# Feed-forward in two phases, with the gated tensor kept in DRAM between them

## What is computed

```python
def conv_ffn(h, w_up, conv_w, conv_b, w_down):        # h is 1024 x 1024, D_FF = 2816
    u = causal_dwconv(h @ w_up, conv_w, conv_b)       # w_up 1024 x 5632, three taps
    g, val = jnp.split(u, 2, axis=-1)
    return (jax.nn.silu(g) * val) @ w_down            # w_down 2816 x 1024
...
for layer in range(2):
    h = h + mixer(rms_norm(h, ...))                   # layer 0: RG-LRU and attention, layer 1: mLSTM
    h = h + conv_ffn(rms_norm(h, f_norm_g[layer]), f_w_up[layer], ..., f_w_down[layer])
return rms_norm(h, final_norm_g)
```

## Time and profile before

| | us |
|---|---|
| median of 3 runs | 2327.4 |
| lowest, highest | 2326.35, 2329.44 |
| span of the profiled execution | 2324.5 |
| feed-forward of layer 0, first to last matmul | about 484.7 to 1172.7 |
| feed-forward of layer 1 | about 1614.9 to 2303.3 |

### The profile page before, as it was taken

The page is one execution under the profiler, slowest core; times in us unless marked ns, Lnnn a source line. Parts: engine busy times, 40 slices in busy tenths (PEclk is TensorE's granted clock), DMA queues, the critical chain, the costliest instruction groups (busy, mean ns, idle before and its releaser), DMA issues.

```text
span 2324.5 us, 31827 instructions
## 1 busy us (share of the span) xinstructions
PE 2264.2 (97%) x10415; PEld 1844.0 (79%) x10415; DVE 1334.6 (57%) x2179; ACT 903.4 (39%) x1595; POOL 1029.8 (44%) x713
## 2 busy tenths in 40 slices
PE   8999998999999999999999999999999999999997
PEld 6776777878888888888878878878888888888885
DVE  6946655268655555555661115664975555555556
ACT  5635554134333333333431124451443333333333
POOL 2314433423555555555533332223345555555554
PEclk9999999999999999999999999999999999999998
DMA  5100001301111111111231110021101111111112
GB/s 179 44 19 1 1 0 30 125 28 46 55 55 55 54 49 45 51 54 54 64 127 46 45 36 28 28 100 55 46 19 55 55 55 54 54 47 51 47 54 91
DMA packets 34583, 122.07 MB, mean 53 GB/s; under 512 B 3840, under 2 KB 3968, under 8 KB 34240
## 3 DMA queue, kind: packets, MB, share of 16 engines
q1 hardware_dynamic: 31616, 106.44, 14.8%
q10 hardware_dynamic: 2880, 14.49, 1.6%
HBM read 112.52 MB, written 8.39 MB: 52 GB/s over the span
## 4 chain that ended last, share of the span: by engine, by line
PE 79%; DVE 8%; ACT 4%; issue 3%; POOL 3%; DMA 2%; ACTq 0%; SPq 0%; DVEq 0%; POOLq 0%
PE ps L736 8%; PE ps L738 8%; PE ps L737 8%; PE ps L818 7%; PE ps L816 7%; PE ps L814 7%; PE ps L854 6%; PE ps L856 6%; PE ps L855 6%; PE ps L1573 2%; DMA stage<-in_wt 2%; POOL wlo L516 2%; PE ps L1738 1%; PE ps L1740 1%; PE ps L1742 1%
## 5 line engine op out<-in xcount | busy, mean ns | idle before, releaser
L516 POOL TENSOR_TENSOR wlo<-stage,whi 128x512 fp32r<-128x512 f32 x308 | 397.3, 1295 | 460.3 <-ACT whi L979 455.7
L736 PE MATMUL ps<-ahi,whi 128*128 128x512 f32 x896 | 368.5, 411 | 17.7 <-DVE alo L2263 10.4
L435 POOL TENSOR_TENSOR whi<-stage,cons 128x1024 fp32r<-128x1024 f32 x64 | 124.5, 1945 | 540.0 <-PE ps L738 329.1
L738 PE MATMUL ps<-ahi,wlo 128*128 128x512 f32 x896 | 351.3, 392 | 0.0
L737 PE MATMUL ps<-alo,whi 128*128 128x512 f32 x896 | 351.0, 392 | 0.0
L1239 DVE TENSOR_TENSOR hT<-hT,ps 128x512 f32<-128x512 f32 x352 | 238.4, 684 | 157.6 <-PE ps L856 157.6
L979 ACT CAST whi<-stage 128x512 fp32r<-128x512 f32 x308 | 189.1, 620 | 357.9 <-POOL stage L529 182.7
L854 PE MATMUL ps<-hid_hi,whi 128*128 128x512 f32 x640 | 251.8, 393 | 2.9 <-POOL wlo L516 1.9
L856 PE MATMUL ps<-hid_hi,wlo 128*128 128x512 f32 x640 | 249.2, 389 | 0.0
L855 PE MATMUL ps<-hid_lo,whi 128*128 128x512 f32 x640 | 249.1, 389 | 0.0
L814 PE MATMUL ps<-ahi,whi 128*128 128x512 f32 x608 | 236.5, 389 | 0.0
(11 more groups left out here) (323 smaller groups left out, 4083.0 us busy)
## 6 DMA issues: line engine op xcount, KB each, us to landing
stage<-in_wt SPq DMA_DIRECT2D x184, 512.0 KB, 3.7
hT<-in_xt SPq DMA_DIRECT2D x16, 256.0 KB, 6.9
hT<-in_xt ACTq DMA_DIRECT2D x8, 512.0 KB, 7.7
spill<-hT ACTq DMA_DIRECT2D x1, 4096.0 KB, 12.1
hT<-spill ACTq DMA_DIRECT2D x8, 512.0 KB, 8.4
out<-hT SPq DMA_DIRECT2D x16, 256.0 KB, 2.1
wqb_s<-in_wqb ACTq DMA_DIRECT2D x1, 1024.0 KB, 4.9
wlru_s<-in_wlru SPq DMA_DIRECT2D x1, 512.0 KB, 10.7
```

The costliest lines, as they stand in the source:

```text
L516: nc.gpsimd.tensor_tensor(block_lo(c), src, block_hi(c).bitcast(F32), ALU.subtract).then_inc(sem(L + "b_ready"), 1)
L736: nc.tensor.matmul(bank, hi, rhs_k[0][:, tok], start=k_first, stop=False)
L738: return nc.tensor.matmul(bank, lo, rhs_k[0][:, tok], start=False, stop=k_last)
```

## The change

The feed-forward block is made in two phases, in both layers. In the **first** (f = 0 to 3 plain, PF = 4, then 18 steps i of seven products, f = i + 4) only up projection, convolution and gate run. The gated tensor of a pair g, two tiles by two token halves (X11, X12, X21, X22), gets four differences in Strassen's way (`hidden_sums`; XT3 overwrites X12), and the seven pieces `hs` are written to DRAM (`hidden_out`, 1792 KB) into `hops`. `first_down`, `down` and `last_down` are gone. In the **second** phase the down projection runs as seven block products p, each over the 11 pairs: 77 steps n = 11p + g. A step takes one 512-wide weight block and one 512-token piece, and makes 12 matmuls into four PSUM banks, which stay open over the 11 steps of the product, and over several products where these share sums: product 1's banks go on through products 2, 3 and 4, product 5's through 6. After each product DVE adds the four banks to a quarter of `hT` (`evacuate`). Per step SP brings the piece (256 KB) from DRAM through a ring of 8, ACT rounds the weight block and the piece (`down_block`, `operand_hi`), POOL takes the weight's rest (`block_rest`), DVE the piece's (`operand_lo`); both splits go through rings of 4. The weight sums S1 to S4 are made by DVE in place (`weight_sum`), at the steps given by `sums_at`. Raw quarters of the down weights are loaded during products 0 to 1. The stage gets a second pair of tiles. The next norm's first half (tokens 0 to 511) is done within products 5 and 6, its second half begins there; layer 1's first two weight tiles are split by POOL at steps 58 and 62. The loops are unrolled.

```diff
-PLAIN = 8
-DOWN_BANKS, LAST_BANKS = (4, 5, 6), (4, 5, 0, 6)
-BLOCKS = 18 * (FG - 2) + 11
+PF = 4
+PLAIN = 2 * PF
+SF = FT - PF
+UPS = 7 * SF
+STEPS = 7 * FG
+BLOCKS = UPS + STEPS
...
-                nc.tensor.matmul(bank, block_hi(b)[:, wk], hid_hi[:, j, tok], start=(j == 0), stop=False)
-                nc.tensor.matmul(bank, block_hi(b)[:, wk], hid_lo[:, j, tok], start=False, stop=False)
-                return nc.tensor.matmul(bank, block_lo(b)[:, wk], hid_hi[:, j, tok], start=False, stop=(j == 1))
-                    for j in range(2):
-                        mm = down_part(g, q, c, n, n // 2, n % 2, j)
-                        mm.then_inc(b_used, 2)
-                    else:
-                        mm.then_inc(sem(L + "down"), 1)
...
+        hops = nc.dram_tensor("hops", (FG * P, 7 * HALF), F32, kind="Internal").ap()
...
+        steps = [("A12", X21), ("A11", X11), ("S2", XT2), ("S3", XT3), ("A22", XT4), ("S1", XT1), ("S4", X22)]
+        targets = [(0, 0), (0, 0), (0, 1), (4, 1), (4, 0), (4, 1), (0, 1)]
+        chain_banks = [(1, 0, 2, 3)] + 4 * [(4, 5, 6, 7)] + 2 * [(1, 0, 2, 3)]
+        fresh = (0, 1, 5)
...
+        sums_at = {}
+        for g in range(FG):
+            sums_at.setdefault(FG + g + 3, []).extend([("S1", g), ("S2", g)])
+            sums_at.setdefault(2 * FG + g + 3, []).append(("S4", g))
+            sums_at.setdefault(3 * FG + g - 2, []).append(("S3", g))
+        sums_made = [what for n in sorted(sums_at) for what in sums_at[n]]
...
+            def hidden_out(L, g):
+                sp.wait_ge(*counts(L, "h_sum")(4 * (g + 1)))
+                sp.dma_start(hops[g * P:(g + 1) * P, :], hs[:, :, :].rearrange("p a b -> p (a b)")
+                             ).then_inc(sem("h_out"), 16)
+            def hidden_in(L, n):
+                g, what = n % FG, steps[n // FG][1]
+                sp.wait_ge(sem("h_out"), 16 * (FG * LAYER[L] + g + 1))
+                sp.dma_start(x_piece(n), hops[g * P:(g + 1) * P, what * HALF:(what + 1) * HALF]
+                             ).then_inc(x_landed(L, n)[0], 16)
...
+                for n in range(XRING, STEPS):
+                    k = n - XRING
+                    sp.wait_ge(*counts(L, "x_lo")(k + 1))
+                    hidden_in(L, n)
+                    if k < FG:
+                        sp.wait_ge(*b_ready(UPS + k + 1))
+                        raw_in(L, t0, "A11", k)
+                    elif k < 2 * FG:
+                        sp.wait_ge(*b_ready(UPS + k + 1))
+                        raw_in(L, t0, "A21", k - FG)
+                        raw_in(L, t0, "A22", k - FG)
...
+                if i == 0:
+                    pe.wait_ge(sem("t_lo"), t_count(L, "t4", 3))
+                pe.wait_ge(*uv(5 * i + 2))
+                product(q + 4, 2, "T4", False)
+                pe.wait_ge(*ev(2 * i + 1))
+                product(q + 5, 0, "B21", False)
+                pe.wait_ge(*uv(5 * i + 3))
+                product(q + 6, 3, "B22", False)
...
+            def down_step(n):
+                p, g = n // FG, n % FG
+                pe.wait_ge(*b_ready(UPS + n + 1))
+                pe.wait_ge(*counts(L, "x_lo")(n + 1))
+                hi, lo = x_hi[n % 4][:, :], x_lo[n % 4][:, :]
+                for m in range(4):
+                    if g == 0:
+                        if p == 0:
+                            pe.wait_ge(*(uv(5 * SF - 1), ev(2 * SF), uv(5 * SF - 1), uv(5 * SF))[m])
+                        elif p == 1:
+                            pe.wait_ge(*counts(L, "prod")(2 * FT))
+                        elif p == 5:
+                            pe.wait_ge(*dn(4))
+                        else:
+                            pe.wait_ge(*dn(4 * (p - 1) + m + 1))
+                    wm = slice(m * P, (m + 1) * P)
+                    bank = ps[:, chain_banks[p][m], :]
+                    nc.tensor.matmul(bank, block_hi(UPS + n)[:, wm], hi, start=(g == 0 and p in fresh), stop=False,
+                                     skip_group_check=True)
+                    nc.tensor.matmul(bank, block_hi(UPS + n)[:, wm], lo, start=False, stop=False,
+                                     skip_group_check=True)
+                    mm = nc.tensor.matmul(bank, block_lo(UPS + n)[:, wm], hi, start=False, stop=(g == FG - 1),
+                                          skip_group_check=True)
+                    if g == FG - 1 and m < 3:
+                        mm.then_inc(sem("down"), 1)
+                mm.then_inc(sem("b_used"), 1)
...
+            for n in range(STEPS):
+                down_step(n)
+                if n == 5 * FG + 9:
+                    pe_sums(pe, next_norm, 0, sq)
+                if n == 6 * FG + 2:
+                    pe_spread(pe, next_norm, 0, diag)
+            pe.sem_inc(w_used, 3 * FT - PLAIN)
...
+            def operand_hi(n):
+                act.wait_ge(*b_used(UPS - 2 if n < 4 else UPS + n - 3))
+                act.wait_ge(*x_landed(L, n))
+                nc.scalar.copy(x_hi[n % 4][:, :], x_piece(n)).then_inc(sem("x_hi"), 1)
...
+            for n in range(4, STEPS):
+                p, g = n // FG, n % FG
+                down_block(n)
+                operand_hi(n)
+                if p == 5 and 3 <= g <= 6:
+                    square(2 * g - 6, 0)
+                    square(2 * g - 5, 0)
+                if (p, g) == (5, 10):
+                    act_std(act, next_norm, 0)
+                if p == 6 and 3 <= g <= 10 and next_norm != "nf":
+                    act_round(act, next_norm, g - 3)
+                if p == 6 and 4 <= g <= 7:
+                    square(g - 4, 1)
+            for pos in range(4, KT):
+                square(pos, 1)
...
+            def prod(f, s):
+                dve.wait_ge(*counts(L, "silu")(f * 2 + (1 + s)))
+                dve.wait_ge(*counts(L, "conv")(tap_count(f, 1, s)))
+                nc.vector.tensor_tensor(x_at(f, s), x_at(f, s), ps[:, 6 + s, :], ALU.mult
+                                        ).then_inc(sem("prod"), 1)
+            def hidden_sums(g, ns):
+                for n in ns:
+                    dve.wait_ge(*(counts(L, "prod")(4 * g + 4) if n == 0 else counts(L, "h_sum")(4 * g + n)))
+                    out, a, b = ((XT1, X12, X11), (XT3, X22, X12), (XT2, X22, XT1), (XT4, X21, XT2))[n]
+                    nc.vector.tensor_tensor(hs[:, out, :], hs[:, a, :], hs[:, b, :], ALU.subtract
+                                            ).then_inc(sem("h_sum"), 1)
...
+            def operand_lo(n):
+                dve.wait_ge(*counts(L, "x_hi")(n + 1))
+                nc.vector.tensor_tensor(x_lo[n % 4][:, :], x_piece(n), x_hi[n % 4][:, :].bitcast(F32), ALU.subtract
+                                        ).then_inc(sem("x_lo"), 1)
...
+                mix(i, 0)
+                if odd:
+                    hidden_sums(f // 2 - 1, (0, 1))
+                mix(i, 1)
+                if i == 0:
+                    for k in range(4):
+                        t4_lo(k)
+                if odd:
+                    hidden_sums(f // 2 - 1, (2, 3))
+                mix(i, 2)
...
+            def weight_sum(kind, g):
+                a11, a12, a21, a22 = (raw[name][g][:, :] for name in ("A11", "A12", "A21", "A22"))
+                if kind == "S1":
+                    dve.wait_ge(*raw_landed(L, g, 4))
+                    out, a, b, op = a21, a21, a22, ALU.add
+                elif kind == "S2":
+                    dve.wait_ge(*counts(L, "made")(made("S1", g)))
+                    dve.wait_ge(*b_ready(UPS + FG + g + 1))
+                    out, a, b, op = a11, a21, a11, ALU.subtract
+                elif kind == "S4":
+                    dve.wait_ge(*counts(L, "made")(made("S2", g)))
+                    out, a, b, op = a12, a12, a11, ALU.subtract
+                else:
+                    if g >= 2:
+                        dve.wait_ge(*b_ready(UPS + 3 * FG + g - 1))
+                    out, a, b, op = d3_tmp[g % 2][:, :], a22, a11, ALU.subtract
+                nc.vector.tensor_tensor(out, a, b, op).then_inc(sem("made"), 1)
...
+            def evacuate(p, m):
+                k0, s = targets[p]
+                if m < 3:
+                    dve.wait_ge(*counts(L, "down")(3 * p + m + 1))
+                else:
+                    dve.wait_ge(*b_used(UPS + (p + 1) * FG))
+                h = hT[:, k0 + m, halves[s]]
+                nc.vector.tensor_tensor(h, h, ps[:, chain_banks[p][m], :], ALU.add).then_inc(sem("down_read"), 1)
...
+            for n in range(4, STEPS):
+                p, g = n // FG, n % FG
+                operand_lo(n)
+                if p >= 1 and g == 2:
+                    for m in range(4):
+                        evacuate(p - 1, m)
+                for kind, of in sums_at.get(n, ()):
+                    weight_sum(kind, of)
+                if (p, g) == (5, 4):
+                    dve.wait_ge(*counts(L, "down_read")(4 * p))
+                if p == 5 and 4 <= g <= 7:
+                    for pos in (2 * g - 8, 2 * g - 7):
```

(13 more changed lines are left out.)

906 lines of the change are left out of this document (391 added, 515 removed).

## The result

| | before | after |
|---|---|---|
| median, us | 2326.9 | 2362.6 |
| lowest, highest, us | 2325.5, 2329.4 | 2357.9, 2363.2 |
| span of the profiled execution, us | 2324.5 | 2360.3 |
| ratio, 95% interval | | 1.015 (1.0138 to 1.0162) |

The account below looks back on a forecast made before the run. TensorE was taken as the bound: 2324.5 - 69.2 + 17.4 + 4 + 14.2 + 14.3 + 5 = 2310.2 us of span, and with 2.9 more, 2313. The 8-in-10 range was 2272 to 2341.

Parts of the forecast that it names:

- seams between up and down: Up-to-down seams in the feed-forward disappear, 11 per layer at 0.35 to 0.37 us: -8 us.
- begin of layer 1: TensorE's wait at layer 1's begin shrinks as first token half's pieces are ready; second half still awaits last adds: -2 us.
- start of products: Step 0 of the products, both layers: TensorE waits for T4's lo parts, a take-out and a block, 8.7 per layer: +17.4 us.
- hidden differences in the steady steps: Steady first-phase steps: second mix behind two `hidden_sums` is done 0.5 us early, so no cost; bound 16 us in all.
- boundaries between products: Second phase: TensorE waits for adds at p = 2 (2.6), 3 (0.9), 4 (0.5), 6 (3.1): +14.2 us, bounds 4 and 24.
- product 6, layer 0: From step 69, norm and operand splits loop through ScalarE and VectorE, losing 13.3 us, plus about 1 for GpSimd's splits: +14.3.
- half clock: TensorE's granted clock falls after waits, about 1.3 us each; four such places allowed: +5 us, bounds 0 to 12.
- T4 wait: Sign of being right: in step 0 of each layer, a TensorE gap of 6 to 9 us released by VectorE's T4 lo part.
- C: Rival: VectorE becomes the bound in product 1 and to step 24, about 40 above the forecast, 2345 to 2353 us; chance 0.14.
- B: Rival: most new waits of TensorE stay hidden, about 20 us added, 2278 us, span 2265 to 2298; chance 0.23.
- D: Rival: transfers late in steps 19 to 29; DMA as bound at 200 GB/s adds 13 per layer, 2339 us; chance 0.05.
- E: Rival: the change doesn't do what it says, shown by a longer matmul pitch; 1% is 13 us; chance 0.06.

Follow-up runs that it names:

- e2: Changed kernel with the weight sums S1 and S2 made on 8 of 512 columns only, leaving out needed work: 2346.6 us, ratio 1.0072.
- e3: Changed kernel with the next norm's sums, spread, squares, rounding and rests put in a lag inside products 5 and 6, same work: 2325.6 us, ratio 0.9985.
- e9: Changed kernel with all reorderings together, mainly mended by the fourth take-out ahead of step 0's last two hidden differences: 2298.8 us, ratio 0.9870.
- e10: e9 with each pair's DRAM write split in two transfers and the four hidden differences one behind each take-out: 2286.7 us, ratio 0.9824.

## Why the prediction was wrong

The sum went from a span of 2324.5 to one of 2310.2; the measured span is 2360.3. By its own steps, in us for both layers:

| step | forecast | measured |
|---|---|---|
| matmuls | -54.4 | -54.4 (10415 to 10175, distance 0.2267 in both) |
| seams between up and down | -8 | gone; not measured apart |
| begin of layer 1 | -2 | +4.5 (begin -1.0, second half +5.5) |
| end | -4.8 | -3.3 (last matmul to end 21.25, now 17.96) |
| start of products | +17.4 | +14.7 |
| hidden differences in the steady steps | 0 | +5.3 |
| into phase 2 | +4 | +5.0 |
| boundaries between products | +14.2 | +26.3 |
| squares in product 5, layer 0 (3.1 of it with GpSimd's split) | none | +5.7 |
| product 6, layer 0 | +14.3 | +8.4 |
| half clock | +5 | about +15 |

With the forecast's -8 for the seams the right column sums to +19, where the spans differ by 35.8. Of the other 17 some 12 are distances around the waits: the one that holds a wait is 0.16 us longer than wait and pitch, and the next one 0.1 to 0.35 longer than the pitch; there are some 40 more such waits than before. Some 4 are the first token half's sums and spread, by estimate, which now take TensorE's own time, and 1.6 lie ahead of the feed-forward. Given the records that are missing, that accounts for the span to within some 2 us.

**The step that failed most is the one on the boundaries**, p = 2 and p = 6. The mechanism was right: adds that stand behind three lo parts. Two sizes were off: the sum had 2.6 and 3.1 us, and both waits are 5.6, where the signs of being right said gaps of 1 to 3. At p = 2 I had VectorE at 3.0 us per step, which is what it takes (3.03), but gave it a lead with which the eleven long steps would leave it only 2.6 late; it has none left when product 1 ends, and the wait is twice two sums and a lo part, 4.92 (1009.09 to 1014.01), and the first add, 0.68: 5.6. Of that lead 2.31 us in layer 0 and 2.54 in layer 1 went to the wait for raw weights in step 14, a term that the sum had at nothing. By an estimate from these rows, 5.6 less 2.3 to 2.5, the wait would be 3.1 to 3.3 us without it, near the 2.6 of the sum; no run shows this. With that wait in place e2 comes down to 0.6, so it isn't enough by itself. At p = 6 I took 3.1 for `act_std`; it is 5.6, since three lo parts of 1.4 to 1.8 (beside four GpSimd rests that run one behind the other) and the diagonal's 1.56 come behind it on VectorE.

**A step that wasn't there at all:** the squares in product 5 make the same circle between ScalarE and VectorE that I had worked out for product 6. I took them as work that fits on average. And the half clock: I allowed four places at 1.3 us. There are nine, and each costs 1.2 to 2.9 us with its first distance: the ten distances from 607.10 to 611.53 take 4.43 us instead of 2.27, and the fourteen from 2308.84 on take 2.9 us too much. Both this term and the boundaries came out beyond their own stated bounds (12 and 24).

**Layer 1's begin** was a term with the wrong sign. I had the first token half ready, as it is (0.83 us of wait in place of 1.87), and did not follow the second half, whose pieces came 2.04 us apart while TensorE needs one in 1.36.

**What was right.** The two faults that the forecast named, orders with a wait at a known place and the loop of product 6, are there. The T4 wait, 6.68 us, lies in the 6 to 9 that was named for it. Product 6 of layer 0 has the waits for lo parts that were named, five of 1.2 to 1.8 us; they cost 8.4 and not 13.3; two of the seven are only 0.3 and 0.5, behind stretches in which the half clock had slowed TensorE. The sharing of VectorE and GpSimd was read rightly off.

**The rivals.** C, VectorE as the bound in steps 14 to 24, was priced at an interval of 1.7 for each operation; one of the three in a step meets a GpSimd instruction, as argued against it, and the step takes 3.03, under the 3.3 from which I had it decide. That point was the mistake: below it no lead covered the rest, and 5.6 us and the half clock came at 3.03 already. B, most waits hidden, didn't occur: each of its places has a wait. D, late transfers, occurred in small, and not where it was looked for: TensorE never waited for a DMA in the second phase, but VectorE did, in step 14. E, a longer pitch, didn't occur. The range's upper end, 2341, came from C and D; no case had three or four terms too small at once, which is what happened. One slip in the text on record: of the tiles that were made in Strassen's way before, only f = 3 became plain, not f = 2 and 3; the count of 2820 is right.

## What to carry to other kernels

An engine that is 61% busy on average can be over its pace for eleven steps, and what stands behind it in its queue then waits for the whole backlog: look up how far the engine leads where the slow stretch ends, not what it does on average. Where two engines each wait once per step for the other's result of the same step, the step costs the sum of both, and a lag of one step in one of the two orders removes it with the same work (some 14 of e3's 37 us). The DRAM write of a single buffer is a wait for its next writer; VectorE has it in the changed kernel too (4 times, 8.0 us), and it reached TensorE only when the waits ahead of it had gone (e9, e10). When a sum comes out right in total, look up whether its parts did (e10).

## What was not expected of the hardware

With GpSimd next to idle in the second phase (e6) the kernel is 44 us faster, of 2363, though GpSimd itself is nearly never what TensorE waits for: in the changed kernel it stands with 4.9 us over both layers. Most of the price of its 154 weight rests is paid by VectorE's lo parts, 1315 ns instead of 734. And a TensorE wait of 5.6 to 6.7 us costs 1.5 to 2.9 us more behind it, at a granted clock of 0.50, a quarter to a half of the wait itself; even after waits of 1.84 us the clock fell twice in product 6 (0.50 from 1174.8 to 1177.8 us).
